# A new order of the heads' instructions across steps, with the output norm and the operand split moved into the loop

## The chip, the cores and the metric

The kernel runs on one core of a Trainium2 chip. The engines are named as in the profile: PE (matrix products), PEld (its weight loads), DVE (vector), ACT (activations and copies), POOL and SP (here only a DMA queue). Each engine works through its own list in order; semaphores tie the lists together. The metric is the device time of one execution in microseconds (us), lower is better.

## The reference

One layer of a streaming encoder runs on 1024 prompt frames with 16 meta tokens ahead of them, and on 64 sample frames. All matrices are float32.

```python
proj = rms_norm(x, norm1) @ w_in                        # 1024 -> 2560 columns, split over two groups of heads
# A: 8 RWKV-7 heads of 64; for each token, state S of 64 x 64:
S = S * w_t + (S @ a_t) b_t^T + v_t k_t^T;   y_t = S r_t
y = group_norm(y) * lnx_w + lnx_b
out_r = (y + sum(r * k * r_k) * v) * (sigmoid(gl) @ g2)
# B: 8 query / 2 kv heads; keys of 2 chunks of 64 and 16 meta tokens, relative bias, softmax with a sink
out_a = rms_norm(softmax(q k^T * SCALE + bias, sink) @ v, attn_out_norm)
h = x + concat(out_r, out_a) @ w_out                    # 1024 -> 1024
y = h + square(relu(rms_norm(h, norm2) @ w_up)) @ w_down  # 1024 -> 4096 -> 1024
```

The outputs are y of the frames (not of the meta tokens), the final states, and the cached rows.

## The kernel before

All activations lie with features on the 128 partitions and tokens along the free dimension: T = 1152 columns = 48 columns of padding, 16 meta tokens, 1024 frames, 64 sample frames, or NT = 9 tiles of 128 (two chunks of 64 each). A large product is split in three: each operand is a rounded upper part (`_hi`) and the rest (`_lo`), and `three_pass` (L101 to L103) adds hi*hi, hi*lo and lo*hi in PSUM. GROUPS cuts the columns into three: (48, 336 wide), (384, 384 wide), (768, 384 wide).

The program has five stages, with a barrier of all engines between them:

1. `phase_project` makes `proj` (20 units of 128 features).
2. `phase_heads` / `loop_heads` computes the heads tile by tile. Step j holds, for the RWKV heads, a chunked form: the matrix of `pairs` "ab" is masked by DVE (L1317), POOL adds the identity (`inverse_start`, L1535), and five levels double the block size of a triangular inverse: `product` on PE (names p1 to p5, L800), `level` on DVE (L1333, L1336, a masked copy out of PSUM), `extend` on PE (e1 to e4, L815; t1 to t5, L819), copies to X and XT on ACT (L1074). Then come `apply` (wu, L884), `transfers` (q, tg, L900 to L917), `read_inner` and `read_state` (y), and two `state_step`s (st0, st1, L925) with DVE adding Gm to each (L1407). The attention of the tile has two halves: `scores` s0, s1 (L837), `logits` on DVE, `probs` on ACT, `normalise` on DVE (L1367 to L1371), `turn_probs` pt, pm (L847, L851), `attend` o0, o1. Preparations of tile j+1 (z, kk, ab, ak, bon) and the group norm of tile j-1 (`out_mean`, `centre`, `squares`, `out_var`, `rstd`, `normed`, `finish`, `out_gate`) stand between. The lists of PE, ACT, DVE and POOL are written out by hand in four functions `step(j)`; SCHEDULE says in which PSUM bank each product lands, in PE's order. Before step 0, a preparation of tile 0 and `Setup.scalar` (copies, and eight output DMAs issued by ACT) run.
3. `mix_heads` squares and sums the attention heads, normalises them, and splits both groups' outputs into mix_hi and mix_lo for all columns. SP fetches the first two column blocks of w_out here (`out_fetch`).
4. `project_out`: for each group g and block m, 24 products and the residual x (as products with the identity); ACT and DVE split w_out (L1764, L1780); the second norm follows.
5. `mlp`: 16 blocks of 256 hidden features, each with `up` and `down`.

The order of the attention's two ops that matter for PE is, on DVE (before.py):

```python
                dve.tensor_tensor(sm[:], sm[:], sk[:], ALU.add).then_inc(den_ok.sem, 1)
                dve.wait_ge(den_ok.sem, den_ok.n(j, e))
                dve.reciprocal(sm[:], sm[:]).then_inc(rec_ok.sem, 1)
                dve.wait_ge(rec_ok.sem, rec_ok.n(j, e))
                dve.tensor_tensor(Lg[:], Lg[:], sm[:].unsqueeze(2).to_broadcast([P, 4, 144]), ALU.mult).then_inc(p_ok.sem, 1)
```

PE transposes Lg (L847) as soon as this is done, in the same step.

Of the kernel before, what the change touches and what calls it, by code (L numbers as in the profile page):

```python
# [12 lines left out]
P = 128  # L13
D_MODEL, SEQ, N_META, DEC_SEQ = 1024, 1024, 16, 64
HD = 64
# [9 lines left out]
GROUPS = [(PAD, 384 - PAD), (384, 384), (768, 384)]  # L25
FF = 4 * D_MODEL
# [22 lines left out]
def build_program(nc, i, o):  # L49

    with ExitStack() as whole:
# [25 lines left out]

        projected = whole.enter_context(ExitStack())
        proj = sb("proj", [P, NU, T], F32, projected)

# [3 lines left out]
        def col(name, t=0, n=1):  # L84
# [4 lines left out]
                 w_stage=w_stage, bank=bank, psum=psum, col=col, bias=bias,  # L89
# [6 lines left out]
        phase_block(nc, i, o, s, projected.close)  # L96
# [360 lines left out]
def phase_heads(nc, i, o, s):  # L457
# [3 lines left out]
    with ExitStack() as ctx:  # L461
# [7 lines left out]
        sink, sink8 = buf("sink", [P, 4]), buf("sink8", [P, 8])  # L469
# [13 lines left out]
        Tr, Gm, Qm = buf("Tr", [P, 2, 4, 64]), buf("Gm", [P, 2, 4, 64]), buf("Qm", [P, 2, 4, 64])  # L483
        Ha, Hb, Hs, Hp = (buf(f"H{n}", [P, 4, 64]) for n in "absp")
        ys, yq = buf("ys", [P, 512]), buf("yq", [P, 512])

# [3 lines left out]
        Lg, PT, PTm = buf("Lg", [P, 4, 144]), buf("PT", [P, 512]), buf("PTm", [16, 512])  # L490
        nm, sm, sk = buf("nm", [P, 4]), buf("sm", [P, 4]), buf("sk", [P, 4])
# [3 lines left out]
        loop_heads(nc, s, v, setup, i, o)  # L495


class Setup:
# [30 lines left out]
    def vector(self, dve):  # L529
        dve.wait_ge(self.sink_in.sem, 16)  # L530
        for hl in range(2):
            rows = slice(64 * hl, 64 * hl + 64)
            last = dve.tensor_scalar(self.v["sink"][rows], self.v["sink8"][rows].rearrange("p (r x) -> p r x", x=2)[:, :, hl],
                                     -1.0, None, ALU.mult)
        last.then_inc(self.sink_ok.sem, 1)
# [9 lines left out]
    def scalar(self, act):  # L545
        o, v, bank = self.o, self.v, self.s["bank"]

        act.wait_ge(self.last_t.sem, self.last_t.n(0))
        act.activation(self.last_rows, bank[0][0:2 * RT, 0:P], ACT.Copy).then_inc(self.last_c.sem, 1)
# [4 lines left out]
        for b in range(2):  # L554
            act.wait_ge(self.kv_t.sem, self.kv_t.n(b))
            dst = self.kvo[b]
            act.activation(dst[:, 0:P], bank[1 + b][:, 0:P], ACT.Copy)
            act.activation(dst[0:64, P:2 * P], bank[1 + b][0:64, P:2 * P], ACT.Copy)
            act.activation(dst[0:16, 2 * P:3 * P], bank[1 + b][0:16, 2 * P:3 * P], ACT.Copy).then_inc(self.kv_c.sem, 1)
# [6 lines left out]
        act.activation(v["vmt"][:], bank[2][0:16, 2 * P:3 * P], ACT.Copy)  # L566
        act.wait_ge(self.st_t.sem, self.st_t.n(0))
        act.activation(v["Hs"][:].rearrange("p a b -> p (a b)"), bank[6][:, 0:256], ACT.Copy)
        act.activation(v["ksm"][:], bank[3][:, 0:80], ACT.Copy).then_inc(self.st_c.sem, 1)

    def tensor(self, pe):
        bank, proj, ident, last_p = (self.s[k] for k in "bank proj ident last_p".split())
        pe.transpose(bank[0][0:2 * RT, 0:P], last_p[:].rearrange("p a b -> p (a b)"), ident[:]).then_inc(self.last_t.sem, 1)
        for b, u in enumerate((K_AT, V_AT)):
            pe.transpose(bank[1 + b][:, 0:P], proj[:, u, S0 - P:S0], ident[:])
            pe.transpose(bank[1 + b][0:64, P:2 * P], proj[:, u, S0:T], ident[:])
            pe.transpose(bank[1 + b][0:16, 2 * P:3 * P], proj[:, u, PAD:64], ident[:]).then_inc(self.kv_t.sem, 1)
        pe.wait_ge(self.st_in.sem, 16)
        pe.wait_ge(self.ck_in.sem, 32)
        for p in range(4):  # L580
            pe.transpose(bank[6][:, 64 * p:64 * p + 64], self.states[:, P * p:P * p + P], ident[0:64, 0:64])
        pe.transpose(bank[3][:, 0:80], self.ck, ident[0:80, 0:80]).then_inc(self.st_t.sem, 1)
# [4 lines left out]
SCHEDULE = [("x", 6, 0), ("zw", 7, 1), ("za", 4, 1), ("p1", 0, 0), ("tr_a", 5, 0), ("tr_b", 6, 0), ("e1", 0, 0), ("t1", 2, 0),  # L587
# [6 lines left out]

# [31 lines left out]
class Fills:  # L626


    def __init__(self, sem, banks):
        self.sem = [(sem(f"bank_full{b}").sem, sem(f"bank_read{b}").sem) for b in range(8)]  # L630
        self.home = {name: b for name, b, _ in SCHEDULE}
        self.banks = banks
        self.count, done = {}, [0] * 8
        for j in range(-1, NT + 1):
            for name, b, off in SCHEDULE:
                if 0 <= j + off < NT:
                    done[b] += 1
                    self.count[name, j + off] = done[b]

    def bank(self, name):  # L640
        return self.banks[self.home[name]]

    def full(self, name):
        return self.sem[self.home[name]][0]

    def read(self, name):
        return self.sem[self.home[name]][1]
# [1540 lines left out]
```

## Time and profile before

| | us |
|---|---|
| runs | 1666.37, 1667.67, 1672.18 (median 1667.67) |
| the profiled execution | 1662.17 |
| its span, first to last instruction | 1660.0 |
| PE / PEld / DVE / ACT / POOL busy | 1517.0 / 1423.6 / 777.5 / 575.4 / 125.8 |

The span is cut below at places where the work changes: 282 (projection over), 318.48 (PE's product "x" of step 0), 646.40 ("x" of step 8), 691.04 (the heads' last instruction), 721.11 (first product of `project_out`), 870 (about where `mlp` begins). One row of a window gives, for each engine, its busy time in the window and, in brackets, the number of instructions; PEclk is the granted clock as a share of 2.4 GHz. In rows of the timeline the first two numbers are the start and the duration in us, and square brackets hold the idle time of the engine just before and what ended it.

### The profile page before, as it was taken

Reading aid. Unit: us, or ns where it says so; the run is one execution under the profiler, and the core shown is the slowest. Engines: PE = TensorE matmul, PEld = TensorE weight load, DVE = VectorE, ACT = ScalarE, POOL = GpSimd, SP = SyncE. Lnnn points to the kernel's source line nnn. Section 1 sums busy time; section 2 is a strip of 40 time slices with the busy share of each in tenths; the row PEclk is TensorE's granted clock in tenths of the full one; section 3 lists DMA queues with packets and bytes.
Section 4 is the critical chain, followed back from the end, with each engine's and each line's share of the span. In section 5 each row is a group of like instructions: output and inputs, shape, how many; then the busy total and the mean of one; then the engine's idle time right before and its main releaser. Section 6 shows DMA issues by size and latency. Waiting matters only on the chain. (4 is left out here: it accounts for less than half of the span.)

```text
span 1660.0 us, 37219 instructions
## 1 busy us (share of the span) xinstructions
PE 1517.0 (91%) x15821; PEld 1423.6 (86%) x15821; DVE 777.5 (47%) x1310; ACT 575.4 (35%) x1126; POOL 125.8 (8%) x131
## 2 busy tenths in 40 slices
PE   6999998578888888569999999999999999999998
PEld 6999997466666666369988999999999999999998
DVE  5124333567777776451252444333344433334444
ACT  6443121355555554531134222233222223322211
POOL 3000000222222222200000000000000000000000
PEclk9999999699999999879999999999999999999999
DMA  6111110000000000142011111111111111111003
GB/s 180 39 48 38 51 38 19 21 4 3 3 3 4 3 4 4 34 116 75 26 52 51 51 51 35 43 51 42 34 51 51 27 48 51 37 39 51 26 1 108
DMA packets 82531, 66.82 MB, mean 40 GB/s; under 512 B 14929, under 2 KB 74507, under 8 KB 82411
## 3 DMA queue, kind: packets, MB, share of 16 engines
q1 hardware_dynamic: 79939, 64.26, 13.0%
q8 instruction: 97, 1.59, 0.4%
q10 hardware_dynamic: 2408, 0.76, 0.2%
q14 instruction: 23, 0.19, 0.0%
q0 software_dynamic: 64, 0.03, 0.0%
HBM read 59.66 MB, written 5.44 MB: 39 GB/s over the span
## 5 line engine op out<-in xcount | busy, mean ns | idle before, releaser
L101 PE MATMUL psum<-mix_hi,uw_hi 128*128 128x384 f32 (+1 forms) x768 | 256.2, 334 | 6.6 <-DVE uw_lo L1983 6.6
L2003 DVE TENSOR_TENSOR hT<-hT,psum 128x384 f32<-128x384 f32 (+1 forms) x384 | 197.2, 535 | 131.7 <-PE psum L103 131.7
L101 PE MATMUL psum<-u_hi,dw_hi 128*128 128x384 f32 (+1 forms) x768 | 255.5, 333 | 3.6 <-DVE dw_lo L1988 3.6
L102 PE MATMUL psum<-mix_lo,uw_hi 128*128 128x384 f32 (+1 forms) x768 | 255.6, 333 | 0.0
L103 PE MATMUL psum<-mix_hi,uw_lo 128*128 128x384 f32 (+1 forms) x768 | 255.3, 332 | 0.0
L102 PE MATMUL psum<-u_lo,dw_hi 128*128 128x384 f32 (+1 forms) x768 | 253.6, 330 | 0.0
L103 PE MATMUL psum<-u_hi,dw_lo 128*128 128x384 f32 (+1 forms) x768 | 253.6, 330 | 0.0
L1995 DVE TENSOR_TENSOR u_lo<-xn,u_hi 128x384 fp32r<-128x384 f32 (+1 forms) x96 | 52.0, 542 | 309.8 <-ACT u_hi L1954 309.8
L101 PE MATMUL psum<-x_hi,w_hi 128*128 128x384 f32 (+1 forms) x480 | 160.4, 334 | 0.3 <-DVE x_lo L328 0.3
L102 PE MATMUL psum<-x_lo,w_hi 128*128 128x384 f32 (+1 forms) x480 | 158.5, 330 | 0.0
L103 PE MATMUL psum<-x_hi,w_lo 128*128 128x384 f32 (+1 forms) x480 | 158.4, 330 | 0.0
L101 PEld LDWEIGHTS psum<-mix_hi,uw_hi 128*128 128x128 f32 x768 | 145.8, 190 | 7.5 <-DVE uw_lo L1983 7.5
L101 PEld LDWEIGHTS psum<-u_hi,dw_hi 128*128 128x128 f32 x768 | 145.1, 189 | 5.7 <-DVE dw_lo L1988 3.9
L102 PEld LDWEIGHTS psum<-mix_lo,uw_hi 128*128 128x128 f32 x768 | 146.3, 190 | 0.0
L103 PEld LDWEIGHTS psum<-mix_hi,uw_lo 128*128 128x128 f32 x768 | 146.2, 190 | 0.0
L102 PEld LDWEIGHTS psum<-u_lo,dw_hi 128*128 128x128 f32 x768 | 145.2, 189 | 0.0
L103 PEld LDWEIGHTS psum<-u_hi,dw_lo 128*128 128x128 f32 x768 | 145.1, 189 | 0.0
L1936 ACT ACTIVATE dw_hi<-d_stage 128x1024 fp32r<-128x1024 f32 x32 | 32.1, 1051 | 313.0 <-PE psum L103 313.0
L1946 ACT ACTIVATE sq<-psum 128x384 f32<-128x384 f32 (+1 forms) x96 | 45.8, 477 | 225.1 <-PE psum L103 224.4
L101 PEld LDWEIGHTS psum<-x_hi,w_hi 128*128 128x128 f32 x480 | 90.6, 189 | 1.3 <-DVE x_lo L328 0.6
L102 PEld LDWEIGHTS psum<-x_lo,w_hi 128*128 128x128 f32 x480 | 90.6, 189 | 0.7
L103 PEld LDWEIGHTS psum<-x_hi,w_lo 128*128 128x128 f32 x480 | 90.6, 189 | 0.0
(273 smaller groups left out, 2378.9 us busy)
## 6 DMA issues: line engine op xcount, KB each, us to landing
w_stage<-in_w_up SPq DMA_DIRECT2D x32, 512.0 KB, 4.4
d_stage<-in_w_down SPq DMA_DIRECT2D x32, 512.0 KB, 4.1
w_stage<-in_w_in SPq DMA_DIRECT2D x16, 512.0 KB, 3.8
proj<-in_x SPq DMA_DIRECT2D x9, 512.0 KB, 5.1
xs<-in_x SPq DMA_DIRECT2D x9, 512.0 KB, 4.5
w_stage<-in_w_in SPq DMA_DIRECT2D x8, 256.0 KB, 4.4
w_stage<-in_w_out SPq DMA_DIRECT2D x8, 256.0 KB, 3.1
w_stage<-in_w_out SPq DMA_DIRECT2D x16, 128.0 KB, 3.4
```

The costliest lines, as they stand in the source:

```text
L101: pe.matmul(out, hi, x_hi, start=first, stop=False)
L102: pe.matmul(out, hi, x_lo, start=False, stop=False)
L103: return pe.matmul(out, lo, x_hi, start=False, stop=last)
L1936: act.activation(dw_hi[:, h], d_stage[:, h], ACT.Copy).then_inc(dwh.sem, 1)
L1946: act.activation(relu[:, e, 0:n], bank[k][:, 0:n], ACT.Relu).then_inc(up_read.sem, 1)
L1995: dve.tensor_tensor(u_lo[:, q, h, c:c + n], u32[:, e, 0:n], u_hi[:, q, h, c:c + n].bitcast(F32), ALU.subtract).then_inc(u_lo_ok.sem, 1)
L2003: dve.tensor_tensor(hT[:, m, c:c + n], hT[:, m, c:c + n], bank[j % 6][:, 0:n], ALU.add).then_inc(dn_add.sem, 1)
```

## The change

- The four lists of `loop_heads` are written anew. A round g (12 of them, -1 to 10) now holds work of four tiles: preparations of g+1, the inverse of g, and of g-1 the attention, the transfers, the state and the read-out; of g-2 the last steps of both norms. The PE's order is that of the new SCHEDULE (below), with `inner_state` ahead of st0, `read_inner` behind it, and `read_state` (y) between x and st1. Each product over two banks is now one entry, read by one instruction of 512, 576 or 1024 elements a partition where there were two.
- st0 and st1 now collect the inner part of the state in PSUM (`inner_state`), so Gm goes, and the states leave PSUM by ACT copies (`half_state`, `state`) in place of DVE adds. ktok is copied by ACT (`k_turned`) in place of DVE. The copy of elc moves from POOL to DVE. The four `tensor_scalar`s of the group norm's affine part stay on DVE, as `affine`.
- The sink becomes a 145th column of the logits, so the small DVE ops on nm and sk, the add to sm and ACT's exponential of sk go. Exponentials are written to Ex in place of Lg.
- `mix_heads` goes. Its work is done tile by tile in the rounds: `out_square`, `out_squares` (osum, four products of 128 columns), `out_rstd`, `out_scale`, and the split by `upper_r`, `upper_a` (ACT) and `lower_r`, `lower_a` (POOL) into `split`, which lies on the same memory as `proj`. The split is spread over units of it (HI, LO); units no longer read (SPARE) hold x, the staged w_down, and two small buffers of `mlp`.
- `out_fetch` of the first two blocks moves into `project_out`.
- GROUPS is replaced by TAIL_GROUPS in `project_out` and `mlp`: the meta tokens' 16 columns are left out there, so the first group is 320 wide.
- Setup: its transposes use other banks, and `Setup.scalar` is called within ACT's `key_rstd(0)`, ahead of `decay(0)`, which DVE's `sides(0)` waits for; before, it came behind all of ACT's preparations. `pairs` "ak" and the bonus of tile 0 now come behind x of step 0.

The core of the diff:

```diff
+M0 = PAD + N_META
+TAIL_GROUPS = [(M0, 384 - M0), (384, 384), (768, 384)]
...
+        projected.close()
+        split = sb("split", [P, NU, T], F32R)
...
-        phase_block(nc, i, o, s, projected.close)
+        phase_block(nc, i, o, s)
...
+SCHEDULE = [("s1", 2, 2, -1), ("tg", 4, 2, -1), ("osum", 1, 1, -2), ("q", 6, 2, -1), ("pt0", 2, 2, -1), ("z", 4, 2, 1),
+            ("st0", 0, 1, -1), ("st1", 1, 1, -1), ("y", 6, 2, -1), ("x", 4, 1, 0), ("p1", 3, 1, 0), ("bon", 7, 1, 0),
+            ("tr_a", 2, 1, 0), ("e1", 3, 1, 0), ("t1", 6, 2, 0), ("ak", 0, 2, 0), ("p2", 4, 2, 0), ("tr_v", 3, 1, 0),
+            ("kk", 6, 1, 1), ("e2", 4, 2, 0), ("mean", 7, 1, -1), ("s0", 2, 2, 0), ("t2", 0, 2, 0), ("p3", 6, 2, 0),
+            ("o0", 5, 1, -1), ("e3", 6, 2, 0), ("tr_b", 4, 1, 0), ("t3", 0, 2, 0), ("p4", 2, 2, 0), ("pt1", 6, 2, -1),
+            ("var", 4, 1, -1), ("e4", 2, 2, 0), ("zz", 1, 1, 0), ("t4", 6, 2, 0), ("p5", 2, 2, 0), ("o1", 0, 1, -1),
+            ("t5", 4, 2, 0), ("ab", 2, 2, 1), ("vt", 7, 1, 0), ("wu", 4, 2, 0), ("tr_k", 0, 1, 0), ("gate", 6, 1, -1)]
+
+
+ROUNDS = range(-1, NT + 2)
...
+            def out_squares(j):
+                pe.wait_ge(osq_ok.sem, osq_ok.n(j))
+                for p in range(4):
+                    mm = pe.matmul(f.bank("osum")[:, 0:P], ones[:], osq[:, P * p:P * p + P], start=p == 0, stop=p == 3)
+                mm.then_inc(f.full("osum"), 1)
...
+            def inner_state(j):
+
+                f.await_read(pe, "tr_k", j)
+                f.await_room(pe, "st0", j)
+                f.await_room(pe, "st1", j)
+                for p in range(4):
+                    at = slice(64 * p, 64 * p + 64)
+                    for hp, e in tiles:
+                        pe.matmul(f.bank(f"st{e}")[half(hp), at], btok[half(e), of_head(p, hp)], WU[half(e), 4 * hp + p, 64:P], start=p == 0, stop=False)
+                    for hp, e in tiles:
+                        mm = pe.matmul(f.bank(f"st{e}")[half(hp), at], ktok[half(e), of_head(p, hp)], vtok[half(e), of_head(p, hp)], start=False, stop=False)
+                mm.then_inc(sums.sem, 1)
...
+            def k_turned(j):
+                f.await_full(act, "tr_k", j)
+                act.activation(ktok[:], f.bank("tr_k"), ACT.Copy).then_inc(f.read("tr_k"), 1)
+            def out_square(j):
+                f.await_read(act, "o1", j)
+                act.activation(q4(osq[:]), o_in(j), ACT.Square).then_inc(osq_ok.sem, 1)
+            def out_rstd(j):
+                f.await_full(act, "osum", j)
+                act.activation(ors[:], f.bank("osum")[:, 0:P], ACT.Ln, bias=eps[:, 0:1], scale=1.0 / 512).then_inc(f.read("osum"), 1)
+                f.await_read(act, "osum", j)
+                act.activation(ors[:], ors[:], ACT.Exp, scale=-0.5).then_inc(ors_ok.sem, 1)
+            def upper_r(j):
+                f.await_read(act, "gate", j)
+                act.activation(split[:, 4:8, cols(j)], r_in(j), ACT.Copy).then_inc(hir_ok.sem, 1)
+            def half_state(j):
+                f.await_full(act, "st0", j)
+                act.activation(flat((Hb if j < LAST else Hp)[:]), f.bank("st0")[:, 0:256], ACT.Copy).then_inc(f.read("st0"), 1)
+            def state(j):
+                f.await_full(act, "st1", j)
+                act.activation(flat(Ha[:]), f.bank("st1")[:, 0:256], ACT.Copy).then_inc(f.read("st1"), 1)
+            def upper_a(j):
+                act.wait_ge(o_ok.sem, o_ok.n(j))
+                act.activation(split[:, 8:12, cols(j)], o_in(j), ACT.Copy).then_inc(hia_ok.sem, 1)
+            def key_rstd(j):
+                f.await_read(act, "kk", j)
+                act.activation(SQ[:], SQ[:], ACT.Ln).then_inc(kkln_ok.sem, 1)
+                act.wait_ge(kkln_ok.sem, kkln_ok.n(j))
+                act.activation(SQ[:], SQ[:], ACT.Exp, scale=-0.5).then_inc(kkrn_ok.sem, 1)
+                if j == 0:
+                    setup.scalar(act)
...
+            def out_scale(j):
+                dve.wait_ge(ors_ok.sem, ors_ok.n(j))
+                for p in range(4):
+                    a = proj[:, 14 + p, cols(j)]
+                    last = dve.scalar_tensor_tensor(out=a, in0=a, scalar=col("an", p), in1=ors[:], op0=ALU.mult, op1=ALU.mult)
+                last.then_inc(o_ok.sem, 1)
...
+            def maximum0(j):
+                f.await_read(dve, "s0", j)
+                dve.tensor_reduce(nm[:], Lg[:], AX_X, ALU.max, negate=True).then_inc(nm_ok.sem, 1)
...
+            def normalise0(j):
+                dve.wait_ge(ex_ok.sem, ex_ok.n(j, 0))
+                dve.reciprocal(sm[:], sm[:]).then_inc(rec_ok.sem, 1)
+                dve.wait_ge(rec_ok.sem, rec_ok.n(j, 0))
+                dve.tensor_tensor(Ex[:, :, 0:144], Ex[:, :, 0:144], sm[:].unsqueeze(2).to_broadcast([P, 4, 144]), ALU.mult)
...
+            def lower_r(j):
+                pool.wait_ge(hir_ok.sem, hir_ok.n(j))
+                pool.tensor_tensor(split[:, 0:4, cols(j)], r_in(j), split[:, 4:8, cols(j)].bitcast(F32), ALU.subtract)
...
+            def lower_a(j):
+                pool.wait_ge(hia_ok.sem, hia_ok.n(j))
+                pool.tensor_tensor(split[:, 14:18, cols(j)], o_in(j), split[:, 8:12, cols(j)].bitcast(F32), ALU.subtract)
...
+HI, LO, SPARE = (4, 5, 6, 7, 8, 9, 10, 11), (0, 1, 2, 3, 14, 15, 16, 17), (13, 18, 19, 12)
...
-def mix_heads(nc, i, s, v):
...
+                for m in range(2):
+                    out_fetch(sp, i, s, m)
...
+                sp.wait_ge(s["wkv_out"].sem, 32)
```

## Rows read from the trace of the kernel before

**Rows 1.** Windows of the span: length, busy us (count) of PE, PEld, DVE, ACT, POOL, PEclk.
```profile
282.00:318.48 36.48, 12.31 (x97) 7.66 (x96) 17.39 (x23) 9.36 (x20) 10.91 (x13) 0.60 0.16 44
318.48:646.40 327.92, 276.20 (x7813) 215.03 (x7812) 245.99 (x451) 182.20 (x429) 86.35 (x88) 1.00 0.01 3
489.32:530.22 40.90, 35.23 (x980) 27.11 (x979) 31.08 (x58) 22.99 (x55) 10.96 (x11) 1.00 0.01 3
646.40:691.04 44.64, 33.92 (x915) 26.09 (x914) 20.32 (x46) 20.27 (x51) 2.53 (x2) 1.00 0.04 9
691.04:721.11 30.07, 3.90 (x7) 1.85 (x7) 22.91 (x30) 19.43 (x28) 9.72 (x3) 0.58 0.17 48
```

**Rows 2.** Waits of PE from 371 to 656, seven steps: total us, times, longest.
```profile
PE psum L847 <- DVE Lg L1371: 26.2, 14, 2.2
PE psum L815 <- DVE Pm L1336: 9.4, 14, 0.9
```

**Rows 3.** Timeline around one handoff in step 4: p5, its mask, t5.
```profile
505.11 0.69 PE L800 MATMUL psum<-X,w_stage 64*64 64x64 f32 x32
...
505.94 0.69 DVE L1336 TENSOR_TENSOR Pm<-psum,lvl 128x512 f32<-128x512 f32 x1 [0.23 <-PE psum L800]
...
506.68 0.69 PE L819 MATMUL psum<-XT,Pm 64*64 64x64 f32 x32
```

**Rows 4.** Groups of instructions from 452 to 615, four steps: busy us, mean ns.
```profile
L1367 DVE TENSOR_TENSOR sm<-sm,sk 128x4 f32<-128x4 f32 x8 | 7.5, 938 | 0.0
...
L1543 POOL TENSOR_TENSOR ys<-ys,yq 128x512 f32<-128x512 f32 x4 | 5.4, 1355 | 14.2 <-ACT yq L1168 14.2
...
L1424 DVE COPY ktok<-psum 128x512 f32<-128x512 f32 x4 | 2.7, 681 | 0.0
L1074 ACT ACTIVATE ys<-psum 128x256 f32<-128x256 f32 x8 | 2.6, 381 | 4.4 <-PE psum L952 4.4
L769 PE MATMUL psum<-ident,kh 128*128 128x128 f32 x16 | 2.6, 287 | 0.0
```

**Rows 5.** Timeline of the preparation of tile 0.
```profile
302.31 0.25 ACT L549 ACTIVATE ys<-psum 28x128 f32<-28x128 f32 x1
...
308.43 0.21 ACT L569 ACTIVATE ksm<-psum 128x80 f32<-128x80 f32 x1
...
310.00 1.99 PE L779 MATMUL psum<-AR,Bt 64*64 64x128 f32 x32 [13.36 <-DVE AR L1302]
...
318.48 1.91 PE L789 MATMUL psum<-id,w_stage 64*64 64x64 f32 x32
```

**Rows 6.** Timeline from the heads' end to the first product of project_out.
```profile
690.35 0.69 DVE L1388 TENSOR_TENSOR proj<-ys,psum 128x512 f32<-128x512 f32 x1
692.47 4.09 SPq L1664 DMA_DIRECT2D w_stage<-in_w_out  x6
...
721.11 0.65 PE L101 MATMUL psum<-mix_hi,wo_hi 128*128 128x336 f32 x1 [18.34 <-DVE wo_lo L1780]
```

**Rows 7.** The tile w_stage from 690 to 760: ns min/median/max, first and last start.
```profile
L1764 ACT ACTIVATE wo_hi<-w_stage x8: 1040/1050/1061, 718.7 to 747.7; 128x1024 fp32r<-128x1024 f32 x8
L1780 DVE TENSOR_TENSOR wo_lo<-w_stage,wo_hi x8: 1216/1225/1226, 719.8 to 748.8; 128x1024 fp32r<-128x1024 f32 x8
...
DMA to landing us min/median/max: 2.9/3.4/5.8
```

**Rows 8.** Timeline of PE in mlp; every product between these has a row.
```profile
1099.67 0.34 PE L101 MATMUL psum<-mix_hi,uw_hi 128*128 128x384 f32 x1
...
1105.48 0.32 PE L101 MATMUL psum<-u_hi,dw_hi 128*128 128x336 f32 x1
...
1111.10 0.42 PE L101 MATMUL psum<-u_hi,dw_hi 128*128 128x336 f32 x1
```

**Rows 9.** Groups of PE from 700 to 1660; 336-wide rows, one of nine.
```profile
L101 PE MATMUL psum<-mix_hi,uw_hi 128*128 128x336 f32 x256 | 83.2, 325 | 6.6 <-DVE uw_lo L1983 6.6
...
L101 PE MATMUL psum<-mix_hi,wo_hi 128*128 128x336 f32 x64 | 22.9, 358 | 18.3 <-DVE wo_lo L1780 18.3
```

More of the change, by code:

```diff
@@ L686, in cols @@
+    osq, ors, split = v["osq"], v["ors"], s["split"]
+    ones = s["ones"]
     def cols(j, n=P, d=0):
@@ new lines, in turn_probs0, with prep_z @@
+            def turn_probs0(j):
+                f.await_room(pe, "pt0", j)
+                turn_probs(j, 0)
+            def prep_z(j):
+                if j == 0:
+                    pe.wait_ge(setup.lora_in.sem, 32)
+                f.await_room(pe, "z", j)
+                for p in range(4):
+                    at = slice(P * p, P * p + P)
+                    pe.matmul(f.bank("z")[:, at], wa[0:64, at], proj[0:64, 12, cols(j)], start=True, stop=True)
+                    mm = pe.matmul(f.bank("z", 1)[:, at], wa[64:P, at], proj[64:P, 12, cols(j)], start=True, stop=True)
+                mm.then_inc(f.full("z"), 1)
+                if j == 0:
+                    setup.tensor(pe)
@@ new lines, in product1, with prep_bonus, turn_a, extend1 @@
+            def product1(j):
+                f.await_read(pe, "x", j)
+                f.await_room(pe, "p1", j)
+                product(j, 1)
+            def prep_bonus(j):
+                pe.wait_ge(rkk_ok.sem, rkk_ok.n(j))
+                f.await_room(pe, "bon", j)
+                pe.matmul(f.bank("bon"), ones_bd[:], SQ[:], start=True, stop=True).then_inc(f.full("bon"), 1)
+            def turn_a(j):
+                turn(j, "tr_a", AR(j))
+            def extend1(j):
+                f.await_read(pe, "p1", j)
+                pe.wait_ge(xt1_ok.sem, xt1_ok.n(j))
+                extend(j, 1)
@@ new lines, in extend_turned1, with pairs_ak, product2, turn_v @@
+            def extend_turned1(j):
+                f.await_room(pe, "t1", j)
+                extend_turned(j, 1)
+            def pairs_ak(j):
+                f.await_room(pe, "ak", j)
+                pairs(j, "ak", Kt)
+            def product2(j):
+                f.await_read(pe, "e1", j)
+                product(j, 2)
+            def turn_v(j):
+                turn(j, "tr_v", v_in(j))
+            def prep_kk(j):
+                pe.wait_ge(kksq_ok.sem, kksq_ok.n(j))
+                pe.matmul(f.bank("kk"), ones_bd[:], SQ[:], start=True, stop=True).then_inc(f.full("kk"), 1)
@@ L1223, in _ @@
[L1223 to L1237 removed]
+                act.activation(yq[:], yq[:], ACT.Exp, scale=-0.5).then_inc(yrs_ok.sem, 1)
@@ L1238, in _ @@
+            setup.loads(act)
+            for g in ROUNDS:
+                step(g)
+            f.await_full(act, "hp", LAST)
+            states = [proj[0:64, 12, 512 * n:512 * n + 512] for n in range(2)]
             for n, dst in enumerate(states):
-                act.activation(dst, bank[1 - n][0:64, :], ACT.Copy).then_inc(hp_c.sem, 1)
+                act.activation(dst, f.bank("hp", n)[0:64, :], ACT.Copy).then_inc(hp_c.sem, 1)
             for n, (src, name) in enumerate(zip(states, ("wkv_p", "wkv_s"))):
@@ new lines, in affine, with with_bonus @@
+            def affine(j):
+                dve.wait_ge(yn_ok.sem, yn_ok.n(j))
+                for p in range(4):
+                    at = slice(P * p, P * p + P)
+                    last = dve.tensor_scalar(ys[:, at], ys[:, at], col("lnw", p), col("lnb", p), ALU.mult, ALU.add)
+                last.then_inc(yg_ok.sem, 1)
+            def with_bonus(j):
+                dve.wait_ge(yg_ok.sem, yg_ok.n(j))
+                dve.tensor_tensor(q4(ys[:]), q4(ys[:]), k_in(j), ALU.add).then_inc(yb_ok.sem, 1)
```

1477 lines of the change are left out of this document (700 added, 777 removed), and 6 rows, old and new, of the table SCHEDULE.

## The prediction

> **What bounds the kernel now.** I read the windows first, then PE's waits, then timelines of one step, of the preparation and of the stage behind the heads. From 318.48 to 691.04, 372.6 us, PE is busy 276.2 + 33.9 = 310.1 us [rows 1]: this stretch is bound by PE's list and the 62.4 us in which that list stands still. One step lasts 40.90 us, PE busy 35.23, idle 5.67; DVE is busy 31.08, ACT 22.99, POOL 10.96 [rows 1]. The idle time has names: over seven steps PE waits 26.2 us for Lg (the softmax is normalised in the step that uses it) and 9.4 us for Pm [rows 2], 3.7 and 1.3 us a step; the rest are small. Then come 30.1 us in which PE does almost nothing (busy 3.9) [rows 1], the stage `mix_heads` with its barriers. The tail is PE at full pace: in `mlp` products start every 0.156 us when 336 wide (36 in 5.62 us) and every 0.176 us when 384 wide (33 in 5.81 us) [rows 8].
>
> **The sum, term by term.** It is made against the profiled span of 1660.0 us. The runs' median, 1667.67, lies 7.7 us above it, and I add that at the end.
>
> *Preparation of tile 0.* `Setup.scalar` takes ACT from 302.31 to 308.64 [rows 5], and now stands ahead of `decay(0)`. That op is an exponential over 1024 elements; I take 1.1 us (ACT's 1024-element copy takes 1.05 [rows 7]). So el_ok comes at about 309.7, `sides` and `rate_out` follow on DVE (three ops of about 0.69, the length of Pm [rows 3]), and "ab" starts at 311.9 where it started at 310.0. But "ak" and the bonus, which stood between "ab" and "x", now come behind x: x(0) needs ab (1.99), the mask (one op over 1024, 1.3), POOL's identity add (1.36, as its other 512-element ops [rows 4]) and handoffs, and starts at about 316.9 against 318.48 [rows 5]. Gain 1.6; if DVE and POOL collide here 1 us of loss.
>
> *PE's work in the heads.* The products are the same, plus osum: four of 128 columns a tile. Four such transposes of kh have a mean of 0.287 us each [rows 4] and overlap, about 0.5 us together, so 9 x 0.5 = 4.5. Ak and bonus of tile 0 move behind x(0): 2.5 (between 1.4 + 1.1 at full clock and the 4 us from 313.6 that they take now at half clock). Together 310.1 + 7.0 = 317.1 us from x(0) on.
>
> *Idle time in the seven full rounds, x(1) to x(8).* I followed each list by hand through one round of PE work, 35.23 + 0.5 = 35.7 us. The measure of a handoff is p5: it starts at 505.11, DVE's mask at 505.94, t5 at 506.68 [rows 3], so behind the 0.51 us that p5 takes to issue, about 1.1 us must be covered by other products. The new order covers it (lengths by the spacing of the products' starts in the step of 489.32 to 530.22, whose PE work is the 35.23 [rows 1]) with bon and tr_a behind p1 (1.5 us), tr_v and kk behind p2 (1.5), o0 behind p3 (1.2), pt1 and var behind p4 (2.1), o1 behind p5 (1.2). The two of 1.2 leave nothing over. On DVE, which now comes to some 30 us of instructions a round (31.08 less ktok's 0.68, the Gm copies, the adds to the states, and the small softmax ops, plus `out_scale`'s four and longer two-bank ops), the masks of levels 3, 4 and 5 end 0.3 to 0.7 us before PE asks. The softmax no longer stops PE: `normalise0` ends about 3.5 us before pt0, `normalise1` a good half round before pt1. ACT gains `k_turned`, two state copies (0.38 each [rows 4]), one square, two short ops and two upper parts, less the exponentials of sk: about 27 of 36 us. POOL gains two subtractions of 1.3, as its 512-element ops [rows 4]: 13.6. Nothing queued behind a new wait is late by this reckoning: the tightest are `upper_a`, `out_square` and `k_turned` ahead of chain copies on ACT, with 0.4 us or more to spare. So idle is between nothing (all covers hold) and 5.7 (all of today's waits come back elsewhere); it is nearest to a round with Lg's waits gone and half of Pm's left. I take 0.5 us, a round of 36.2 us.
>
> *The first and last rounds* have nothing to fill the gaps of their chain. Round 0 lacks the work of a tile before it: by the same reckoning x(0) to x(1) takes 32.3 us, of which 5.4 is idle. From x(8) on there are the rest of tile 8's inverse, then its softmax, read-out, both norms and the splits in a row: 49.1 us where 44.64 pass today [rows 1], because ACT's `upper_a`, POOL's `lower_a` and the copies and DMAs of the final states come last. Idle there is about 7.5. The heads end at 316.9 + 32.3 + 7 x 36.2 + 49.1 = 651.7, against 691.04: gain 39.3 with the preparation. (By the other account, 317.1 of work plus 5.4 + 3.5 + 7.5 of idle time gives 333.5, within 1.5 of the 334.8 that stand here.)
>
> *Behind the heads.* Today 30.07 us pass from the heads' last instruction to the first product [rows 1, 6]. In the new program the barrier (691.04 to 692.47, 1.4 us [rows 6]) is followed at once by `out_fetch`: three issues of 0.68 (six take 4.09 [rows 6]), a landing 3.4 us after the third [rows 7], ACT's split 1.05 and DVE's 1.22 [rows 7]: 9.2 us. Gain 20.9. What hid that fetch was `mix_heads`; with its cover gone it is paid in full and already counted. The later fetches keep today's pace of four us a block of 24 products. SP's wait for the states' DMAs stands behind the first nine issues; it has nothing left to wait for.
>
> *The tail.* A 336-wide product becomes 320 wide. From 0.156 and 0.176 us at 336 and 384 columns, 16 columns are 6.7 ns. There are 3 x (256 + 256 + 64) = 1728 of them [rows 9]: 11.5 us; between nothing (if something other than columns held the 336-wide ones) and 11.5. The slope between the two widths says columns: 11.3.
>
> Sum: 39.3 + 20.9 + 11.3 = 71.5, a span of 1588.5. With 7.7: **1596 us**.
>
> **DVE against POOL.** The add of sm and sk, four elements a partition, takes 938 ns in the mean [rows 4], 0.8 us more than so small an op needs: it stands behind one of POOL's. POOL gets 2.6 us more work a round, and most DVE ops of a round have both operands in SBUF. If DVE stood still for all of POOL's 13.6 us, a round would be 30 + 13.6 = 43.6 us on DVE alone, with a span of 1588.5 + 7 x 7.4 = 1640 and a time of 1648, to which I give 0.01 of the 0.07 of rival 2; half of that, which is nearer to today's rows (some 3 us a step), gives 36.8. The Trainium skill speaks of this in "SBUF — State Buffer", section "Who interferes with whom": a vector instruction with two SBUF inputs and a GpSimd instruction that reads SBUF exclude each other, and whichever starts second waits until the first is done. By that rule each of POOL's ops can hold DVE for its full length, which would make the 43.6 the worst case; the row of sm agrees with it.
>
> **Rivals.**
> 1. *The round is set by handoffs, not by PE's work.* DVE is late by a POOL op at one or two of the five masks, each with 0.3 to 0.7 us to spare: 0.85 us a collision, two to four a round, a round of 38 to 40 us. For it: DVE's list is 30 of 36 us and strictly in order. Against: the masks read PSUM, and POOL is idle for most of a round. Span 1601 to 1615, time 1609 to 1623.
> 2. *The old waits come back whole,* at other places: round 40.9, span 1588.5 + 7 x 4.7 = 1621, time 1629. The change of order then does nothing, and what is left is the stage that goes and the narrower tail. Against it: the largest wait, Lg's, has a round of slack.
> 3. *The tail does not narrow:* time 1607.
> 4. *Slower.* The one loop that could cost so much: POOL's `normed(g-1)` waits for ACT's `rstd`, which waits for PE's var; DVE's `affine` waits for `normed`, and behind `affine` stand the mask of ab, POOL's `inverse_start` and so x of the next round. By hand the loop has 8 us of slack. It would have to be 8 + 10.2 = 18 us late in every round to eat the 71.5 us (71.5 / 7 = 10.2); at 20 us late the time is 1596 + 7 x 12 = 1680. The ops in that loop last 8 us in all.
>
> **Chances.** Forecast (a round of 35.7 to 37.6 us) 0.62, rival 1 0.22, rival 2 0.07, rival 3 0.06, slower or no change 0.03. What a measurement of this kernel can tell from no change is about 0.3%, 5 us. Faster holds all but the last: 0.97; same 0.01; slower 0.02. The forecast's own range is 1586 (no idle time in full rounds, last rounds 6 us shorter) to 1607. The range takes in most of rival 1 and all of rival 3: low 1580, another 6 us for the ends of the heads that I reckoned; high 1620.
>
> **What the profile after would show.** A period of x in the full rounds of 35.7 to 37.6 us with PE's waits for the transposed softmax (its line of `turn_probs`) gone; if it is 38 to 40, waits of PE for Pm or X and long four-element or SBUF-only DVE ops beside POOL's. X(0) at about 317. About 9 us from the heads' last instruction to the first product of `project_out`. Products of 320 columns starting every 0.149 us. The prediction fails if DVE or ACT shows a busy share near 95% in the rounds, if x(8) to the heads' end takes far more than 49 us, or if the first blocks of w_out arrive late.

## The result, and the profile after

| | us |
|---|---|
| kernel before, median (range) of 4 runs | 1669.77 (1666.37 to 1672.18) |
| changed kernel, median (range) of 4 runs | 1574.68 (1573.90 to 1576.58) |
| ratio, 95% interval | 0.9434, 0.9411 to 0.9456 |
| changed kernel, profiled execution / its span | 1575.04 / 1573.2 |

The changed kernel is 95 us faster. The prediction was 1596 with a range of 1580 to 1620: direction and mechanism held, the measured time lies below the range, and the gain was underrated by 21 us. By the prediction's own terms:

| term | predicted | measured | difference |
|---|---|---|---|
| x(0) starts at | 316.9 | 317.68 | +0.8 |
| x(0) to x(1) | 32.3 | 33.16 | +0.9 |
| seven full rounds | 7 x 36.2 = 253.4 | 240.58 (7 x 34.37) | -12.8 |
| x(8) to the heads' end | 49.1 | 48.1 | -1.0 |
| heads' end to the first product | 9.2 | 9.6 | +0.4 |
| tail, first product to the end | 927.6 | 924.1 | -3.5 |
| from the profiled span to the median | 7.7 | 1.5 | -6.2 |

Windows of the changed kernel, with the columns of [rows 1]: the preparation, x(0) to x(8), one full round, the last rounds, and the stretch to `project_out`.

```profile
283.50:317.68 34.18, 10.11 (x80) 6.95 (x79) 13.77 (x19) 9.37 (x21) 5.03 (x7) 0.65 0.18 47
317.68:591.42 273.74, 268.89 (x7780) 217.44 (x7782) 219.18 (x338) 203.37 (x448) 104.16 (x96) 0.99 0.02 4
489.09:523.48 34.39, 34.30 (x997) 27.66 (x991) 28.13 (x45) 26.35 (x59) 13.21 (x12) 1.00 0.02 4
591.42:639.51 48.09, 42.31 (x1046) 32.14 (x1038) 23.85 (x48) 29.56 (x69) 12.40 (x10) 1.00 0.01 3
639.51:649.11 9.60, 0.00 (x0) 0.00 (x0) 1.23 (x1) 1.06 (x1) 0.00 (x0) 0.53 0.63 165
```

In a full round PE now stands still for 0.09 us where it stood for 5.67 [rows 1], and its busy time is lower too, 34.30 against 35.23, though osum was added. DVE fell from 31.08 to 28.13, ACT rose from 22.99 to 26.35, POOL from 10.96 to 13.21. The whole list of PE's waits in the full rounds, which answers to [rows 2], is one line:

```profile
PE psum L791 <- issue: 0.4, 1, 0.4
```

The handoff of [rows 3], p5 to its mask to t5, in the changed kernel:

```profile
508.82 0.68 PE L796 MATMUL psum<-X,w_stage 64*64 64x64 f32 x32
...
509.43 0.65 PE L832 MATMUL psum<-PT,vtk 128*64 128x256 f32 x4
...
509.58 0.69 DVE L1445 TENSOR_TENSOR Pm<-psum,lvl 128x512 f32<-128x512 f32 x1 [1.27 <-PE psum L796]
...
510.01 0.65 PE L834 MATMUL psum<-PTm,vmt 16*64 16x256 f32 x4
510.59 0.69 PE L806 MATMUL psum<-XT,Pm 64*64 64x64 f32 x32
```

The mask still runs 0.76 us behind p5's start. But o1 (L832, L834) fills PE until t5 at 510.59, and DVE was idle for 1.27 us ahead of the mask: it waits for PE, not PE for it.

The preparation, against [rows 5]: x(0) waits last not for POOL's identity (L1691, done at 317.31) but for DVE's read of z(1) (L1499, done at 317.53), whose PSUM bank it takes over.

```profile
309.52 1.04 ACT L1300 ACTIVATE L<-L 128x1024 f32<-128x1024 f32 x1
...
312.63 1.99 PE L778 MATMUL psum<-AR,Bt 64*64 64x128 f32 x32 [11.32 <-DVE Bt L1438]
...
316.05 1.26 POOL L1691 TENSOR_TENSOR w_stage<-w_stage,id 128x512 f32<-128x512 f32 x1 [10.34 <-DVE w_stage L1463]
316.31 1.22 DVE L1499 TENSOR_TENSOR Z<-psum,par 128x1024 f32<-128x1024 f32 x1 [0.41 <-PE psum L887]
...
317.68 1.15 PE L791 MATMUL psum<-id,w_stage 64*64 64x64 f32 x32 [1.42 <-DVE Z L1499]
```

Behind the heads, against [rows 6]: fetch, ACT's split, DVE's split, first product, as reckoned.

```profile
638.85 0.65 ACTq L1418 DMA_DIRECT2D out_wkv_s<-proj  x1
641.32 5.40 SPq L1766 DMA_DIRECT2D w_stage<-in_w_out  x6
646.74 1.06 ACT L1871 ACTIVATE wo_hi<-w_stage 128x1024 fp32r<-128x1024 f32 x1 [8.15 <-DMA w_stage<-in_w_out]
...
647.83 1.23 DVE L1887 TENSOR_TENSOR wo_lo<-w_stage,wo_hi 128x1024 fp32r<-128x1024 f32 x1 [10.86 <-ACT wo_hi L1871]
...
649.11 0.64 PE L106 MATMUL psum<-split,wo_hi 128*128 128x320 f32 x1 [13.28 <-DVE wo_lo L1887]
```

In `mlp`, two products of 320 columns, 33 apart, against [rows 8]: 0.146 us from start to start (predicted 0.149).

```profile
1026.12 0.30 PE L107 MATMUL psum<-u_lo,dw_hi 128*128 128x320 f32 x1
...
1030.95 0.31 PE L107 MATMUL psum<-u_lo,dw_hi 128*128 128x320 f32 x1
```

### The profile page after: what moved, and what is told of

It is laid out like the page before. It is cut to its first block and busy times, and to the rows that moved or that the text cites. A ratio compares the mean times of both kernels' runs of the same rounds, so it can differ in the third digit from the quotient of the medians.

```text
span 1573.2 us, 36686 instructions
## 1 busy us (share of the span) xinstructions
PE 1495.3 (95%) x15887; PEld 1411.4 (90%) x15887; DVE 726.0 (46%) x1165; ACT 587.1 (37%) x1136; POOL 137.9 (9%) x137
## 5 line engine op out<-in xcount | busy, mean ns | idle before, releaser
L106 PE MATMUL psum<-split,uw_hi 128*128 128x384 f32 (+1 forms) x768 | 251.9, 328 | 6.6 <-DVE uw_lo L2091 6.6
L108 PE MATMUL psum<-split,uw_lo 128*128 128x384 f32 (+1 forms) x768 | 251.8, 328 | 0.0
L107 PE MATMUL psum<-split,uw_hi 128*128 128x384 f32 (+1 forms) x768 | 251.6, 328 | 0.0
L2103 DVE TENSOR_TENSOR u_lo<-proj,u_hi 128x384 fp32r<-128x384 f32 (+1 forms) x96 | 51.5, 537 | 300.5 <-ACT u_hi L2062 300.5
L106 PEld LDWEIGHTS psum<-split,uw_hi 128*128 128x128 f32 x768 | 145.4, 189 | 7.5 <-DVE uw_lo L2091 7.5
L2044 ACT ACTIVATE dw_hi<-proj 128x1024 fp32r<-128x1024 f32 x32 | 32.2, 1053 | 311.0 <-PE psum L108 311.0
L107 PEld LDWEIGHTS psum<-split,uw_hi 128*128 128x128 f32 x768 | 145.4, 189 | 0.0
L108 PEld LDWEIGHTS psum<-split,uw_lo 128*128 128x128 f32 x768 | 145.3, 189 | 0.0
L2054 ACT ACTIVATE proj<-psum 128x384 f32<-128x384 f32 (+1 forms) x96 | 45.5, 474 | 216.4 <-PE psum L108 215.7
L241 ACT ACTIVATE proj<-psum 128x384 f32<-128x384 f32 (+3 forms) x60 | 28.6, 478 | 172.1 <-PE psum L108 172.0
```

The lines of the kernel that those rows point to most:

```text
L106: pe.matmul(out, hi, x_hi, start=first, stop=False)
L107: pe.matmul(out, hi, x_lo, start=False, stop=False)
L108: return pe.matmul(out, lo, x_hi, start=False, stop=last)
L241: act.activation(proj[:, bass.ds(u, 1), c:c + n].rearrange("p a n -> p (a n)") if not isinstance(u, int) else proj[:, u, c:c + n], bank[3 ...
L2044: act.activation(dw_hi[:, h], d_stage[h], ACT.Copy).then_inc(dwh.sem, 1)
L2054: act.activation(relu[:, e, 0:n], bank[k][:, 0:n], ACT.Relu).then_inc(up_read.sem, 1)
```

## The experiments

Each was timed beside the kernel before, whose median was between 1663.19 and 1667.35 us there; "after" is the changed kernel, 1574.68 us, which was not timed again beside them. Two variants of it that change next to nothing (the copies back on DVE, the shifted tiles) came within 1.2 us of it; of a difference to after, 1 to 2 us may lie between the sessions.

**PE's list or the handoffs?** The same four products were added to both kernels, ahead of the transposes of the softmax's first half (in before, behind the wait for room and ahead of the wait for the softmax):

```diff
+                for n in range(4):
+                    pe.matmul(f.bank("pt0")[:, P * n:P * n + P], ident[:], ident[:], start=True, stop=True)
```

After with them:

> The kernel after with four more products of 128 columns a round on PE, ahead of the transposes of the first half of the softmax (their results are overwritten). Osum, of the same size, took 1.09 us. If PE's list sets the round: each full round 1.09 us longer (35.5), seven of them 7.6 us, and up to 2 more in the first and last rounds: 1582 to 1585. If handoffs set it (DVE, ACT, POOL with PE waiting for them): below 3 us, 1575 to 1578.

Before with them:

> The kernel before with the same four products a step, put where PE waits 2.2 us for the normalised first half of the softmax. If the chain sets the step there: the products vanish in that wait, within 2 us of the kernel before, the wait 1.1 us shorter. If PE's list sets it: 9.8 us slower.

After: 1582.63 us, 8.0 more. The seven full rounds last 35.43 us in the mean, 1.07 more. The window of one of them, and PE's waits in the full rounds, all of them:

```profile
387.28:422.54 35.26, 35.17 (x1005) 28.53 (x998) 28.19 (x45) 26.31 (x59) 13.21 (x12) 1.00 0.01 3
```

```profile
PE psum L791 <- issue: 0.3, 1, 0.3
```

Before: 1666.30 against 1665.95 us, ratio 1.0015 (0.9998 to 1.0033). The first line of PE's waits there fell from 26.2 to 19.3 us, 0.99 a step:

```profile
PE psum L849 <- DVE Lg L1373: 19.3, 14, 1.6
```

So 1.09 us of PE work costs its full length in each round of after, and in before nothing that could be measured, where nine times 1.09 would be 9.8 us: the change turned a loop set by its chain into one set by PE's list.

**One wait put back.** In after, `normalise0` moved behind `queries_added`, and PE waits for it. With it, `maximum1` comes later too, and `logits1`, which overwrites Lg, gets a wait of its own for the exponentials that read Lg:

```diff
                 f.await_room(pe, "pt0", j)
+                pe.wait_ge(nrm0_ok.sem, nrm0_ok.n(j))
...
                 f.await_full(dve, "s1", j)
+                dve.wait_ge(ex_ok.sem, ex_ok.n(j, 0))
...
-                if 0 <= g - 1 < NT:
-                    normalise0(g - 1)
...
                     transfer_added(g - 1)
+                    queries_added(g - 1)
+                    normalise0(g - 1)
                     maximum1(g - 1)
-                    queries_added(g - 1)
```

> The kernel after with one wait put back: DVE normalises the first half of the softmax behind the additions to Tr and Qm, and PE's transposes of it wait for that. By the timeline of after the transposes then start about 1.8 us late in each full round. Theory one, a stall of PE costs its idle time and another 0.2 us, because the last product before a stall runs to its end (some 0.2 us behind its last issue) and counts as busy: idle 1.8 and busy 34.5 a round, a round of 36.3 to 36.5 us. Theory two, a stall costs its idle time alone: busy stays at 34.3, a round of 36.1 to 36.2. Theory three, the wait is absorbed, since the order leaves room elsewhere: a round below 35 us. Eight rounds carry it: 14 to 17 us slower by one and two, 1589 to 1592. In the kernel before, the granted clock fell to half in one to four steps of the heads in the two later profiles (none in the first), and there a step took 1 to 2.5 us more; if PE's idle time is what brings that, falls of the clock should show in rounds here too, some 2 to 6 us in all. And the multiplication by the reciprocal, which lasts 1.85 us in after and 0.76 in the other half, should last 0.76 away from POOL's operations.

1599.82 us, 25.1 more, beyond all three. The wait is the one foreseen, 1.8 us a round, but five of the full rounds last 37.7 to 38.0 us; the other two, 36.64 and 35.84, are 2.1 and 2.4 longer than the same rounds of after. The line of PE's waits for six of these rounds (353 to 592 us), and two neighbouring rounds, one of each kind:

```profile
PE psum L822 <- DVE Ex L1472: 10.7, 6, 1.8
```

```profile
504.95:542.70 37.75, 35.88 (x996) 28.81 (x990) 27.10 (x45) 26.32 (x59) 12.70 (x12) 0.95 0.02 4
542.70:579.34 36.64, 34.50 (x994) 27.68 (x989) 27.24 (x45) 26.83 (x60) 12.69 (x12) 1.00 0.01 3
```

In the second the clock is full throughout: idle 2.14 us, 1.78 of it the wait. Against the same round of after it has 2.05 us more of idle time and 0.04 more of busy time; the other quiet round has 2.26 and 0.18 more. This is near theory one (2.0 in all), but does not separate it from theory two, since the first of these rounds lasts between 34.32 and 34.71 us in after and in its variants with the same list of PE. In the other round above the granted clock was at its lower level for a while (0.95 in the mean), and it takes another 1.1 us. From x(0) to x(8) 297.42 us pass where after takes 273.74, so a wait of 1.8 us cost 3.0 a round; what the clock takes was underrated. The multiplication lasts 0.76 us there, as expected.

**A second profile of the kernel before.**

> The kernel before, unchanged, profiled a second time. In its first profile the 384-wide products of the tail started every 175 to 176 ns from about 760 to 1100 us and every 173.5 to 174 ns elsewhere, and in the kernel after they start every 173.4 to 174.2 ns throughout. Theory one, the slow spell is an accident of that execution: it is gone here or lies elsewhere, and the span may be 2 to 4 us shorter in the tail. Theory two, it belongs to the kernel before (its operands lie in other memory, or its stage of mixing precedes): 175 to 176 ns at the same place. Either way a step of the heads lasts 40.9 us, and the span is 1658 to 1671 us; where the runs of this kernel differ by 6 us among themselves, the windows of the two profiles should show in which stage.

1667.33 us, span 1665.2. The 5.2 us to the first profile lie in the heads, not in the tail: x(0) to x(8) took 334.09 us at a clock of 0.97 against 328.03 at 1.00 (x(8) of the first profile starts at 646.51; [rows 1] has the window to 646.40). Three of its steps:

```profile
362.70:405.00 42.30, 36.13 (x979) 28.00 (x978) 30.96 (x57) 23.06 (x54) 10.89 (x11) 0.96 0.01 3
405.00:446.30 41.30, 34.75 (x979) 26.95 (x978) 31.16 (x57) 22.98 (x54) 10.94 (x11) 1.00 0.01 3
446.30:487.00 40.70, 34.91 (x979) 27.03 (x978) 31.18 (x57) 22.98 (x54) 10.96 (x11) 1.00 0.01 3
```

Four of its eight steps show a fall of the clock like that of the first of these, none of the first profile's does, and two more profiles show one (the kernel before with the four products above) and three (the one with the narrow tail below). In the full rounds of after and of its eight variants without that wait, the clock falls in none. The slower 384-wide products are back, so the accident is excluded. Grouped by operand they are no spell in time: they are the products that read the mixed operand, mix_hi and mix_lo (`split` in after), 176.1 ns from start to start ([rows 8] show 33 of them in 5.81 us), while `down`'s take 173.5 in the same stretch.

**The tail alone, on both kernels.** `TAIL_GROUPS = GROUPS` in after, and TAIL_GROUPS in the tail of before:

> The kernel after with the first column group 336 wide again in project_out and mlp. Theory of the prediction, a slope between two widths: 1728 products of 6.7 ns more, 11 us slower, about 1586. Theory of the trace of after: a 320-wide product starts every 146.2 ns where a 336-wide one took 155.9, so 1728 x 9.7 ns = 16.8 us are lost, and the waits of PE for the added hT, which came with the narrow group (14 shown in the profile, 2.3 us of idle time, about 0.32 us of lost spacing each, 4.6 us), go away again: 12 us slower, about 1587, with no wait for hT. If narrowing was worth nothing: 1575.

> The kernel before with only the first column group of project_out and mlp narrowed from 336 to 320 columns. If the tail's gain does not depend on the rest of the change: 11 to 13 us faster than the kernel before, a ratio of 0.992 to 0.994, products of 320 every 146 ns, and PE's short waits for hT as in the kernel after. If the kernel after gained 14.8 us in its tail for another reason (where the operands lie, or the freed memory), less than 8 us here.

After with 336: 1584.82 us, 10.1 more. Before with 320: 1657.37 against 1667.12, 9.8 less, ratio 0.9948 (0.9928 to 0.9968). Both fall short of what was expected (11 to 12, and 11 to 13), and the interval of the second, 5.3 to 12.0 us, is wide; but the two agree: the narrow group is worth some 10 us in either kernel, and not the 14.8 by which the tail shrank between the two profiles. The waits for hT (DVE's additions to it free PE's PSUM banks) come with it: two lines of PE's waits in the tail, first after, then before with 320; with 336 there is none.

```profile
PE psum L106 <- DVE hT L2111: 2.3, 14, 0.2
```

```profile
PE psum L103 <- DVE hT L2005: 2.3, 14, 0.2
```

**Where the operands lie.**

> The kernel after with 32 unused columns of float32 (128 bytes a partition) ahead of proj, so that proj, split and every later tile lie 128 bytes further on. Grouped by operand, the slower 384-wide products of the kernel before are those that read the mixed operand alone: 176.1 ns from start to start in all three profiles, against 173.5 for the down products there and 174.0 for the same products in after; its 336-wide ones are quicker (153.4 against 155.9). In before that operand begins 128 bytes past the place, modulo 256, at which every other large operand begins. Theory one, the place in memory decides: here all products show it, 384-wide ones near 176.1, 336-wide ones of the projection near 153.4, 320-wide ones near 146.6, and the time grows by 3456 x 2.2 ns in the tail, 2.1 - 1.2 us in the projection and 0.9 for the 320-wide ones: 9 us, 1583 to 1585. Theory two, it is something else of that tile (its neighbours, who else reads it): 174.0 ns as in after, and 1573 to 1577.

1575.56 us, and the pace is as in after (384-wide 173.5 and 173.9 ns, 320-wide 146.3 to 146.5). Theory one fell: moving everything by 128 bytes does not bring the slower pace. The weights moved along with the mixed operand, though, while in before that operand lies apart from them, on the other side of the memory; its place relative to the weights was not tried. Why the products of the mixed operand were slower in before stays open.

**Did the idle stage slow them?** Twenty copies on DVE ahead of the first split of w_out:

> The kernel after with twenty copies on DVE ahead of the first split of w_out, so that PE stands idle for 15 to 30 us more between the heads and project_out, as it did in the kernel before (30 us). In the three profiles of before 384-wide products start every 175 to 176 ns for 300 to 500 us behind that stage, in the two of after every 173.4 to 174.2. Theory one, the idle gap brings the spell: it shows here too, and the time grows by the gap and 3 to 5 us more. Theory two, it comes from the layout of the operands or from mix_heads itself: 173.4 to 174.2 ns throughout, and the time grows by the gap alone.

1583.10 us, 8.4 more; the first product came at 657.81 in place of 649.11, 8.7 later (the copies took 0.76 us each, less than I had thought). 384-wide products at 173.6 and 173.9 ns: theory two, for a gap of 18 us, where before has 30.

**The copies back on DVE**, in after:

```diff
-                act.activation(ktok[:], f.bank("tr_k"), ACT.Copy).then_inc(f.read("tr_k"), 1)
+                dve.tensor_copy(ktok[:], f.bank("tr_k")).then_inc(f.read("tr_k"), 1)
```

and so for the two states (`k_turned` behind `gated`, `half_state` behind `normalise1`, `state` ahead of `level1`).

> The kernel after with the copies of ktok and of both states back on DVE (1.4 us more on DVE and 1.6 less on ACT in each round), at places where the trace of after shows DVE with time to spare. DVE is busy for 28.1 of a round's 34.4 us and PE stands still for 0.1. If PE's list sets the round and the covers have room: rounds within 0.2 us of 34.4, within 3 us of after, 1573 to 1578. If the engine of these copies is what made the round short: a mask or Hb comes late, 0.5 to 1.4 us a round, 1579 to 1585, with PE's waits for Pm or Hb in the trace.

1575.86 us, the range of its runs (1574.12 to 1577.28) over that of after. One round, in which DVE has 1.1 us more and ACT as much less than in after:

```profile
384.69:419.06 34.37, 34.28 (x995) 27.63 (x989) 29.25 (x48) 25.29 (x55) 13.21 (x12) 1.00 0.01 4
```

In this order it makes no measurable difference which engine makes these copies.

**Two more improvements.** First `setup.scalar` behind `decay(0)`, split into its copies and then its eight stores; then the first block of w_out fetched in the last rounds, into that half of w_stage which `Ab` (the matrix "ab" of a tile, in alternate halves) no longer uses there:

```diff
                 act.activation(flat(L2[:]), flat(L2[:]), ACT.Exp, scale=-1.0).then_inc(el_ok.sem, 1)
+                if j == 0:
+                    setup.scalar(act)
+                    setup.stores(act)
```

> The kernel after with ACT's exponential of tile 0 (decay) ahead of the setup's copies, and the setup's eight stores behind them. In after decay starts at 309.52, 6.25 us behind the end of key_rstd, and DVE waits 5.78 us for it. If that chain sets x of step 0: x starts 5 to 6 us earlier against the end of the projection, 1569 to 1570. If something else is next in line (the copies that pairs ab waits for, POOL's product of r and k, the half clock): 1 to 3 us, 1572 to 1574. That the setup's stores cost nothing where they are: 1575.

```diff
-    Ab = lambda j: Ab2[:, j % 2]
+    Ab = lambda j: Ab2[:, (j + 1) % 2]
...
             setup.sync(sp)
+            f.await_full(sp, "y", LAST - 1)
+            out_fetch(sp, i, s, 0)
```

> The kernel after with the first block of w_out fetched while the last round runs, into the half of w_stage that its tile does not use. In after, 9.1 us pass from the barrier's last instruction to the first product, 5.4 of them until the landing. If the fetch sets that stretch: the first product comes 5 us earlier, but the second block then lands 2 to 3 us after it is wanted, so 3 to 5 us are left, 1570 to 1572. If a later fetch sets the pace of the whole first group: less than 1 us, 1574 to 1575.

> Both of these edits, which lie in different stages: the sum of their gains, 6 to 11 us faster than after, 1564 to 1569. If they share a cover (a later start of the heads absorbs nothing behind them), the sum holds; if not, no more than the larger one, 1569.

The first: 1570.40 us, 4.3 less, just short of what the chain alone would give. The exponential and x(0):

```profile
302.02 1.04 ACT L1302 ACTIVATE L<-L 128x1024 f32<-128x1024 f32 x1
...
311.57 1.15 PE L795 MATMUL psum<-id,w_stage 64*64 64x64 f32 x32 [1.42 <-DVE Z L1504]
```

x(0) is 6.1 us earlier than in after, about 1.2 of it because the projection ended earlier in this execution; the last wait is again that for z(1).

The second: 1572.71 us, 2.0 less, between the two expectations. The first product comes 6.7 us earlier, but what was behind it is late now, the blocks of x and the third block of w_out:

```profile
642.45 0.63 PE L107 MATMUL psum<-split,wo_hi 128*128 128x320 f32 x1 [7.87 <-DVE wo_lo L1888]
650.01 0.49 PE L1917 MATMUL psum<-ident,proj 128*128 128x128 f32 x2 [0.77 <-DMA proj<-in_x]
655.03 0.41 PE L107 MATMUL psum<-split,wo_hi 128*128 128x320 f32 x1 [0.34 <-DVE wo_lo L1888]
```

This takes 2.2 us back. Another 2.3 go around the start of `mlp`, where the granted clock of this execution was lower (0.91 from 748 to 825 us, against 0.96 from 753 to 830 in after).

Both: 1565.45 us (1565.02 to 1567.34), ratio to before 0.9408 (0.9382 to 0.9434), 9.2 less than after, within the 6 to 11 expected though more than the 6.3 of the two alone, and the fastest kernel here.

## Why the prediction was right in kind and short by 21 us

*The step that failed is the round of 36.2 us*, "one round of PE work, 35.23 + 0.5 = 35.7 us" and 0.5 us of idle time on top. It was taken for a floor, and the round went below it, to 34.37 (busy 34.23, idle 0.14): 2.1 us less of PE's old work, 0.6 more for osum, 0.4 less of idle time. Term by term:

- PE's old work: 34.23 less osum's 1.09 is 33.14, not 35.23. Of these 2.1 us, 0.37 is my choice of one step: over the seven steps from 359.43 to 646.51 PE was busy 244.02 us, 34.86 a step, and the step of [rows 1] is longer by one group, ak's products, which took 1.41 us until the next start there and 1.03 in both neighbours. Most of the rest is that busy time was not work. A product ends some 0.18 us behind its last issue (p5: 0.69 us long, its successor starts 0.51 behind it, at 505.62); in a row without gaps the next product covers that, ahead of a stall nothing does, and it is counted as busy. The seven steps have 42 stalls. The last product ahead of each has a record of 218 to 283 ns, where the same products follow each other every 15 to 139 ns in a row: together 1.13 us a step. The wait put back neither confirms nor denies this: for one stall a round it shows 0.04 and 0.18 us more of busy time, within the scatter of rounds. I had the figure in hand, used it for "the 0.51 us that p5 takes to issue", and not for the sum. The Trainium skill, "TensorE: Matmul & The Clock Gate", section "Single matmul latency", has for a bf16 product at full clock a constant of about 166 ns beside its columns; the 0.18 of this trace, of float32 products, lies near it, but is no check on it, since the profile's ends of products are modelled. What is left, 0.6 us, is open. Some groups changed their spacing from before to after with no stall behind them (in the mean of seven, ab 0.18 us less, ak 0.26 less, wu 0.25 more), so which product follows which may matter; that was not tried alone.
- osum: 1.09 us, not 0.5. I priced it by transposes; a product of float32 of that size has two records in the trace where a transpose has one, and takes twice as long. The same size, added once more to every round, cost 8.0 us in all.
- Idle time: 0.14, not 0.5. The covers held, as reckoned. DVE came to 28.13, not 30.

*The 7.7 us from span to median* were a property of the kernel before and not of the measurement: 2.2 lie around the span, and the rest goes with the clock, which in other executions of before falls in some steps of the heads, with 5.7 us or more of idle time a step; over 38 runs of before, time and granted clock have a correlation of -0.81. After has no such idle time, no such fall, and runs 2.7 us apart. With 1.8 in place of 7.7 the forecast would have been 1590.

*The tail:* 14.8 us, not 11.3 (1728 products of 6.7 ns are 11.5), of which the narrow group is some 10 by two experiments. My slope was taken between two widths that read different operands [rows 8]: `up`'s 384 at 0.176 and `down`'s 336 at 0.156. Narrowing took 9.7 ns off `down`'s product (156.0 to 146.3, 768 of them, 7.4 us) and 7.3 off those of the mixed operand (153.4 to 146.1, 960 of them, 7.0), not 6.7; but PE now waits for DVE's hT, 14 times in the profile, where one start comes 0.47 us behind the last in place of 0.15, 4.5 us. That makes 9.9. Another 4.1 come from the mixed operand's 384-wide products (1920 of them, 2.1 ns each), a gain for which the prediction had no term. The 0.8 left are within what one execution differs from another: the same tail lasted 937.1 to 938.9 us in three profiles with that of before, and 923.6 to 926.9 in six with that of after (after, and its variants with four more products, the gap, the shift, the DVE copies and the later setup), so that the gain is 10 to 15 us, 12.4 between the means.

*What held.* The stall for the softmax is gone and did not come back elsewhere (rivals 1 and 2 fell: no wait of PE over 0.4 us in the full rounds). Behind the heads 9.6 us pass for 9.2, the last rounds take 48.1 for 49.1, the preparation gains 2.3 us from the projection's end on (34.2 for 36.5 [rows 1]). The slower loop of rival 4 does not show. Rival 3 fell with the 0.146 us. How the gain divides between the new order and the stage that went is read from the windows (372.6 to 321.8 us from x(0) to the heads' end, 30.1 to 9.6 behind it); no run has one without the other.

*DVE against POOL.* The collisions are there, at places that have room. The two halves of the softmax have the same multiplication, and only the first stands beside a POOL operation; groups of the full rounds, busy us and mean ns:

```profile
L1470 DVE TENSOR_TENSOR Ex<-Ex,sm 128x576 f32<-128x576 f32 x7 | 12.9, 1845 | 0.2
...
L1506 DVE TENSOR_TENSOR Ex<-Ex,sm 128x576 f32<-128x576 f32 x7 | 5.3, 758 | 0.2
```

In one round the first starts at 514.03, 0.04 behind POOL's L1691 (513.99 to 515.26), and ends 0.62 behind POOL's end, nearly the 0.76 that it takes by itself. Moved, in the kernel with the wait put back, it takes 757 ns in each of the full rounds. The Trainium skill's rule ("SBUF — State Buffer", "Who interferes with whom"), that of a vector instruction with two SBUF inputs and a GpSimd instruction that reads SBUF the later waits for the whole of the earlier, agrees with these rows to 0.14 us. The collision costs 1.1 us of DVE a round here and nothing of PE.

## What to carry to other kernels

PE's busy time in a loop that stalls is no floor: take the spacing of starts for its work, not the durations, and count each stall as its idle time, the record of the last product, and what the clock may take. In the loop here, once nothing waited, added products showed in full and a move of 1.1 us between two engines with room showed nothing, so find out which of the two regimes a loop is in (one added product tells) before you price anything. And an offset between the profiled run and the median belongs to a kernel; ask what varies in it before you carry it over.

## What the runs showed of the hardware

- With a stall of 1.8 us once a round the lower clock came in six of eight rounds, and a round took 3.0 us more in the mean; in the full rounds of nine kernels without that stall it came in none. The kernel before stalled for 5.7 us a step in six pieces of 0.2 to 2.2 us, and its clock fell in none, three or four of its steps, depending on the execution (and in one step of the execution with four products added). What decides that stayed open.
- Products of one shape on PE differ by operand: with mix_hi and mix_lo 384 columns take 176.1 ns against 173.5, and 336 columns 153.4 against 156.0, in every profile of kernels that have these tiles and widths. In after, whose mixed operand lies elsewhere, all 384-wide products take 173.5 to 173.9. A shift of all tiles by 128 bytes does not bring the difference, and 8.7 us more of idle time ahead of the stage do not either; the cause is open.
